# Two of three terms of each gate and up product in one 512-column matmul, with other buffers for the first units

## What is computed

```python
        gu = rmsnorm(h, g_ffn[i]) @ w_gate_up[i]      # (512, 2048) @ (2048, 11264)
        g_, u_ = gu[..., :D_FF], gu[..., D_FF:]
        h = h + (jax.nn.silu(g_) * u_) @ w_down[i]    # (512, 5632) @ (5632, 2048)
```

## Time and profile before

| | us |
|---|---|
| median of three runs (2725.11 to 2725.7) | 2725.15 |
| the profiled execution | 2726.73 |
| its span, first to last instruction | 2724.9 |
| TensorE busy | 2687.5 (99%) |
| VectorE busy | 1818.1 (67%) |
| ScalarE busy | 1187.9 (44%) |
| first to last issue of a gate and up weight load | 1125.3 to 1999.6 |

### The profile page before, as it was taken

The page is one execution under the profiler, slowest core; times in us unless marked ns, Lnnn a source line. Parts: engine busy times, 40 slices in busy tenths (PEclk is TensorE's granted clock), DMA queues, the critical chain, the costliest instruction groups (busy, mean ns, idle before and its releaser), DMA issues.

```text
span 2724.9 us, 42137 instructions
## 1 busy us (share of the span) xinstructions
PE 2687.5 (99%) x17284; PEld 2450.5 (90%) x17284; DVE 1818.1 (67%) x2072; ACT 1187.9 (44%) x1527; POOL 169.7 (6%) x130
## 2 busy tenths in 40 slices
PE   9999999999999999999999999999999999999998
PEld 7888888888888888899999999999998999999887
DVE  6555545455565433587787777777788787788745
ACT  5334434334455233354444444444454353444543
POOL 0000000010000111100000000000000000000052
PEclk9999999999999999999999999999999999999999
DMA  6333333323333554454555555555567564553333
GB/s 219 93 93 108 100 100 108 101 85 113 100 97 101 193 200 121 129 161 148 168 155 155 163 148 155 163 162 148 155 216 252 146 208 124 182 153 112 88 98 100
DMA packets 130454, 382.95 MB, mean 141 GB/s; under 512 B 11120, under 2 KB 37872, under 8 KB 127728
## 3 DMA queue, kind: packets, MB, share of 16 engines
q1 hardware_dynamic: 113824, 333.35, 37.3%
q0 software_dynamic: 9792, 34.61, 6.9%
q10 hardware_dynamic: 6672, 12.63, 1.2%
HBM read 301.90 MB, written 44.04 MB: 127 GB/s over the span
## 4 chain that ended last, share of the span: by engine, by line
PE 92%; DVE 4%; DMA 1%; ACT 1%; issue 1%; POOL 0%; ACTq 0%; DVEq 0%; SPq 0%; POOLq 0%
PE ps L574 30%; PE ps L576 30%; PE ps L575 30%; PE ps L648 1%; DVE arena L1948 1%; ACT w_hi L986 0%; DMA arena<-hid 0%; PE ps L637 0%; DVE w_lo L1941 0%; DVE w_lo L1566 0%; DMA raw<-raw 0%; DVE lo L1941 0%; DVE emb L2277 0%; DVE res L2093 0%; PE ps L615 0%
## 5 line engine op out<-in xcount | busy, mean ns | idle before, releaser
L574 PE MATMUL ps<-arena,w_hi 128*128 128x256 f32 (+1 forms) x4164 | 1365.2, 328 | 11.2 <-DVE w_lo L1941 7.5
L576 PE MATMUL ps<-arena,w_lo 128*128 128x256 f32 (+1 forms) x4164 | 1360.0, 327 | 0.0
L575 PE MATMUL ps<-arena,w_hi 128*128 128x256 f32 (+1 forms) x4164 | 1359.7, 327 | 0.0
L986 ACT ACTIVATE w_hi<-raw 128x1024 fp32r<-128x1024 f32 (+1 forms) x536 | 559.9, 1045 | 933.5 <-PE ps L576 914.1
L574 PEld LDWEIGHTS ps<-arena,w_hi 128*128 128x128 f32 x4164 | 793.7, 191 | 83.9 <-issue 12.1
L576 PEld LDWEIGHTS ps<-arena,w_lo 128*128 128x128 f32 x4164 | 793.4, 191 | 66.8
L575 PEld LDWEIGHTS ps<-arena,w_hi 128*128 128x128 f32 x4164 | 793.7, 191 | 65.1 <-issue 0.2
L1566 DVE TENSOR_TENSOR w_lo<-raw,w_hi 128x1024 fp32r<-128x1024 f32 x212 | 268.4, 1266 | 434.1 <-ACT w_hi L986 433.7
L1941 DVE TENSOR_TENSOR w_lo<-raw,w_hi 128x1024 fp32r<-128x1024 f32 (+1 forms) x318 | 379.0, 1192 | 147.1 <-ACT w_hi L986 145.6
L574 PE MATMUL ps<-arena,hi 128*128 128x256 f32 (+1 forms) x1244 | 355.3, 286 | 11.5 <-DVE lo L1941 10.8
L575 PE MATMUL ps<-arena,hi 128*128 128x256 f32 (+1 forms) x1244 | 354.8, 285 | 0.0
(11 more groups left out here) (174 smaller groups left out, 1821.1 us busy)
## 6 DMA issues: line engine op xcount, KB each, us to landing
raw<-w_gu SPq DMA_DIRECT2D x176, 512.0 KB, 4.1
raw<-w_in SPq DMA_DIRECT2D x108, 512.0 KB, 3.5
raw<-w_dn SPq DMA_DIRECT2D x64, 512.0 KB, 4.4
raw<-raw POOLq DMA_DIRECT2D x60, 512.0 KB, 4.7
hid<-res SPq DMA_DIRECT2D x22, 1024.0 KB, 5.2
raw<-w_o SPq DMA_DIRECT2D x32, 512.0 KB, 3.8
raw<-w_pg SPq DMA_DIRECT2D x32, 512.0 KB, 3.7
arena<-hid SPq DMA_DIRECT2D x14, 1024.0 KB, 8.2
```

Of the source, the lines that this page charges most:

```text
L574: mm(out, hi, x[:, 0, :], start=start, stop=False, skip_group_check=more)
L575: mm(out, hi, x[:, 1, :], start=False, stop=False, skip_group_check=more)
L576: return mm(out, lo, x[:, 0, :], start=False, stop=stop, skip_group_check=more)
L986: return nc.scalar.activation(out, in_, ACT.Copy, scale=scale)
```

## The change

For units below 44 a term k is two matmuls instead of three. The high part of the weights is multiplied by both parts of the moving operand at once: 512 columns, which are two runs of 256 columns in the operand's slot (its high and low part lie 8 KB apart), written to a whole PSUM bank. Its left half then holds high x high, its right half high x low. The low part of the weights times the high part of the operand (256 columns) is added to the right half. So the result is the sum of the two halves of a bank. The snapshots and the two sums take whole banks (1024 elements instead of 512), and VectorE adds right to left in two new steps, `gate_fold` and `up_fold` (512 elements each); scale, Silu and product work on the left halves. The rows that a tile needs in `res` are now all its own until `hidden_tile`, so snapshots of unit u wait for the hidden tile of unit u - 2.

Beside it: slots 0, 7, 5, 1 for even and 2, 3, 4, 6 for odd units, with the loads of unit 0 in the order A21, A22, A11, A12; `gate_scale` moves behind `up_sum`, `up_scale` behind `sum_3`, `recip` behind low part 2 of unit 1, Silu behind high part 3; ScalarE scales its half of x_last ahead of the store of h; at the change to down residual tiles 1 and 2 change places; two of four w_pp loads wait for the last unit's block sum 3. The down units keep `product`.

```diff
-    return (0, 1, 2, 3)[i] if v % 2 == 0 else (5, 7, 4, 6)[i]
+    return (0, 7, 5, 1)[i] if v % 2 == 0 else (2, 3, 4, 6)[i]
...
             def block_load(v, i):
+                if v < 2 and raw_slot(v, i) < RAW:
+                    sp.wait_ge(w_lo_done, N_WO + 29 + raw_slot(v, i))
                 if v == 0:
-                    sp.wait_ge(w_lo_done, N_WO + 29 + i)
+                    if i == A21:
+                        sp.wait_ge(mrg_hi, 8)
                 elif v == 1:
                     if i == A22:
                         sp.wait_ge(acc_done, SQUARES[3])
-                    if i == A21:
-                        sp.wait_ge(mrg_hi, 8)
                     if i == A12:
                         sp.wait_ge(tot_done, 4)
...
                 if v == 0:
-                    for i in (A21, A22, A12):
+                    for i in (A21, A22, A11, A12):
                         block_load(0, i)
-                    for i in (A21, A11, A22, A12):
+                    for i in (A11, A21, A22, A12):
                         block_load(1, i)
...
                 if v == FF + 2:
                     sp.wait_ge(hidden, FF)
-                    residual_again(2)
+                    residual_again(1)
                 if v == FF + 1:
                     sp.wait_ge(hidden, FF - 1)
-                    residual_again(1)
+                    residual_again(2)
...
+            def product_by_parts(out, hi, lo, x, start, stop, more):
+
+                mm(out, hi, x, start=start, stop=False, skip_group_check=more)
+                return mm(out[:, 1], lo, x[:, 0], start=False, stop=stop, skip_group_check=more)
...
-                    i = product(out, hi[:, c], lo[:, c], x[:, :, k], j < 4 and k == 0, k == pairs(v) - 1, j >= 4)
+                    if v < FF:
+                        i = product_by_parts(parts, hi[:, c], lo[:, c], x[:, :, k], j < 4 and k == 0,
+                                             k == pairs(v) - 1, j >= 4)
+                    else:
+                        i = product(out, hi[:, c], lo[:, c], x[:, :, k], j < 4 and k == 0, k == pairs(v) - 1, j >= 4)
...
             def snap_row(u):
                 act.wait_ge(s_used, 7 * u + 3)
+                if u == 1:
+                    act.wait_ge(xs_lo, 22)
                 if u >= 2:
-                    act.wait_ge(ff_sum, 2 * (u - 2) + 2)
+                    act.wait_ge(hidden, u - 1)
                 b = bank0(u)
-                copy(halves(ff_row(u, US)), ps[:, b + DELTA:b + GAMMA + 1, LEFT]).then_inc(snap, 1)
+                copy(up_rows(u), ps[:, b + DELTA:b + GAMMA + 1]).then_inc(snap, 1)
...
-                b = bank0(u)
-                tt(halves(ff_row(u, GG)), halves(ff_row(u, GS)), ps[:, b + BETA:b + GAMMA + 1:2, LEFT],
-                   ALU.add).then_inc(ff_sum, 1)
+                b, g = bank0(u), gate_rows(u)
+                tt(g, g, ps[:, b + BETA:b + GAMMA + 1:2], ALU.add).then_inc(ff_sum, 1)
+
+            def gate_fold(u):
+                dve.wait_ge(ff_sum, 2 * u + 1)
+                g = gate_rows(u)
+                tt(g[:, :, LEFT], g[:, :, LEFT], g[:, :, RIGHT], ALU.add).then_inc(g_folded, 1)
```

More of the change, by code:

```diff
@@ L301, in hid_rows, with gate_rows, up_rows @@
             return res[:, 0:4, :] if u // 2 % 2 == 0 else res[:, 12:16, :]
-        def ff_row(u, i):
-            return res[:, 4 + 4 * (u % 2) + i, :]
-        GS, US, GG, UU = range(4)
+        def gate_rows(u):
+            return res[:, 8 - 4 * (u % 2):10 - 4 * (u % 2), :]
+        def up_rows(u):
+            return res[:, 10 - 4 * (u % 2):12 - 4 * (u % 2), :]
         def halves(row):
@@ L523, in _ @@
                     continue
+                block_load(v, A11)
+                if last_before:
+                    fill(last_before, 2)
                 block_load(v, A12)
@@ L863, in _ @@
             i.then_inc(piece_used, 1)
-            def n_group(g, n, pair):
-                free(g, 4)
-                for j in range(4):
-                    piece(n + j, j, 2 * pair, [n_tile(4 * j + k) for k in range(4)], j == 0, j == 3)
-            def down(g, n, pair0, need):
-                pe.wait_ge(ff_lo, need)
-                for d in range(8):
-                    free(g + d, 4)
-                    piece(n + d, d, 2 * ((pair0 + d) % 4), [r1[:, k] for k in range(4)], True, True)
             def strassen(v, j):
@@ L898, in strassen @@
                 pe.wait_ge(s_lo, n + 1)
-                x, out = x_slot(g, j), ps[:, bank0(v) + BANK_OF[j], X_HALF[0]]
+                x, bank = x_slot(g, j), ps[:, bank0(v) + BANK_OF[j]]
+                out, parts = bank[:, X_HALF[0]], bank.rearrange("p (t c) -> p t c", t=2)
                 hi, lo = S_HI[ring(n)], S_LO[ring(n)]
@@ L1398, in _ @@
                     x_split(T3_, SIX, res[:, 0:6, RIGHT], 0, N_WO + 31)
+                if g == 7:
+                    act.wait_ge(emptied, G_E)
+                    copy(x_last[:, 1, :], res[:, 15, :], gn[:, G_FFN + 15:G_FFN + 16]).then_inc(x_made, 1)
                 h_store(g)
                 if g == 7:
-                    copy(x_last[:, 1, :], res[:, 15, :], gn[:, G_FFN + 15:G_FFN + 16]).then_inc(x_made, 1)
                     hi(0, 2)
@@ L1426, in _ @@
                         nc.scalar.preload_act_table(ACT.Silu)
-                    if j == 2 and v <= FF:
+                    if j == 3 and v <= FF:
                         gate_act(v - 1)
@@ L2055, in up_sum, with up_fold @@
                 dve.wait_ge(s_used, 7 * u + 7)
-                b = bank0(u)
-                tt(halves(ff_row(u, UU)), halves(ff_row(u, US)),
-                   ps[:, b:b + 1, LEFT].broadcast_to([P, 2, 256]), ALU.add).then_inc(ff_sum, 1)
+                b, r = bank0(u), up_rows(u)
+                tt(r, r, ps[:, b:b + 1].broadcast_to([P, 2, SEQ]), ALU.add).then_inc(ff_sum, 1)
+            def up_fold(u):
+                dve.wait_ge(ff_sum, 2 * u + 2)
+                r = up_rows(u)
+                tt(r[:, :, LEFT], r[:, :, LEFT], r[:, :, RIGHT], ALU.add).then_inc(u_folded, 1)
             def up_scale(u):
-                dve.wait_ge(ff_sum, 2 * u + 2)
-                tt(ff_row(u, UU), ff_row(u, UU), rstd[:, 0, :], ALU.mult).then_inc(u_scaled, 1)
+                dve.wait_ge(u_folded, u + 1)
+                r = up_rows(u)[:, :, LEFT]
+                tt(r, r, by_token(0), ALU.mult).then_inc(u_scaled, 1)
             def hidden_tile(u):
@@ L2071, in hidden_tile @@
                     dve.wait_ge(h_out, 16 * 8)
-                tt(hid_row(u, u % 2), ff_row(u, GG), ff_row(u, UU), ALU.mult).then_inc(hidden, 1)
+                tt(halves(hid_row(u, u % 2)), gate_rows(u)[:, :, LEFT], up_rows(u)[:, :, LEFT],
+                   ALU.mult).then_inc(hidden, 1)
             def t_1_3(u):
@@ L2141, in _ @@
                 lo(v, 2)
+                if v == 1:
+                    recip(3, 3, 1, 0, D)
                 if v <= FF:
                     up_sum(v - 1)
+                    gate_scale(v - 1)
                 if v >= FF:
```

35 lines of the change are left out of this document (18 added, 17 removed).

## The result

The changed kernel takes 2697.07 us, the median of seven runs, against 2725.11 for the kernel before beside it: a ratio of 0.9916, 95% interval 0.9902 to 0.993. The forecast was 2693 us, the range 2687 to 2706. But the seven runs are no cloud around one value. Four lie between 2694.91 and 2697.07 us, three between 2711.43 and 2712.08, and none in between. The kernel before has nothing like it (2723.91 to 2726.59). Most of what follows is about these 16 us.

The account below looks back on a forecast made before the run. The prediction took TensorE, busy 99% of 2724.9 us, to bound the kernel. From 2725.15 us, -32.8 (joint matmul) - 1.5 (first units) + 2 (last gate and first down unit) = -32.3 gave 2693 us, range 2687 to 2706.

Parts of the forecast that it names:

- TensorE bounds the stretch, and only its own instructions can shorten it: Gate and up stretch, 1200 to 1980 us: TensorE always busy at full clock, nothing waits on its path.
- Joint matmul, -32.8 us: Units below 44: each of 2464 terms falls from 360.0 to 346.7 ns, one matmul's fixed cost; 32.8 us less.
- rival 1: Joint matmul pays inside where its second operand run begins: 2726 us (3%), or 2720 us with 2.5 ns gained a term (3%).
- starts 0.24 us after a joint matmul: Gate stretch, sign of a wrong forecast: this spacing would point to rival 1; 0.23 would show the forecast right.
- VectorE's new work, 0: Gate and up units: longer sums and two folds stay hidden behind TensorE, VectorE 91 to 93% busy; cost 0.
- Rival 2: VectorE's folds and sums run at full lengths without overlap: 4 to 22 us back, 2697 to 2715 us; 10%.
- Rival 3: VectorE becomes the bound, its two-bank reads and folds at nearly twice the time: 21.5 us a unit, 2784 us; 4%.
- First units, -1.5 us: Units 0 and 1: new slots shorten product (0,2)'s wait, later products wait more; -5.0 + 3.5, bounds -5 and +2.
- the clock probably stays: Unit 0, product (0,2): with its wait cut to 2.1 us the clock no longer falls to half, -2.3 us.
- ScalarE's larger snapshots, 0: Gate and up units: about 1 us more per unit on ScalarE, which has room; cost 0.
- Last gate and first down unit, +2 us: Change to down: VectorE's longer work delays low parts 3 to 6 by 1.1 to 1.7 us; bounds 0 and +5.

Follow-up runs that it names:

- the repeat: The changed kernel timed again with no edit: 2696.39 us, ratio 0.991 to the kernel before.
- pair order: Changed kernel with two 512-column, then two 256-column matmuls by turns inside a product of units 1 to 43: 2701.07 us, ratio 0.9909.
- the buffer kernel: Kernel before with only the change's slots, load order and load waits, earlier x_last copy and later w_pp loads: 2723.21 us, ratio 0.9991.
- eight-and-eight order: Changed kernel with eight 512-column matmuls, then eight of 256 columns, in each product of units 1 to 43: 2703.44 us, ratio 0.9922.

## Why the prediction held, and where it did not

**TensorE bounds the stretch, and only its own instructions can shorten it: right.** With three matmuls and all of the change's other work the term stays at 359.9 ns; with the joint matmul it becomes 346.5 or 353.2.

**Joint matmul, -32.8 us: right in the lower group, twice too much in the upper.** 360.0 - 346.5 = 13.5 ns a term is 33.3 us; 360.0 - 353.2 = 6.8 ns is 16.8. The step that failed is "The cost goes with the instruction itself, not with what follows it, so a mixed row of them can be priced from these". The three starts at the norm's total cross the border of the sizes once each way; they show nothing of a row in which every neighbour differs. Such a row has two paces, and the evidence held only the better. The forecast of 2693 is 2 to 4 us below the lower group and the range holds it, but the upper group, 3 of 7 runs here and 2 of 6 in the repeat, lies 5 to 8 us above the range. That the median came out inside is luck: four of seven runs were of the lower group, and with one more of them in the upper it would have been 2711. The thirteen runs of the changed kernel have a mean of 2702.1.
On the fixed cost of a matmul, the runs give 13.5 ns for one merged pair in the faster pace. The 2.5 ns of the Trainium skill's page "TensorE: Matmul & The Clock Gate" ("Wait — 56ns, not 53.3ns?") would have made the gain 6 us, an estimate from that page, and no run here agrees with that: even the slower pace gives 6.8 ns a term.

**The 2720 and 2726 of the first rival: not seen.** Its mechanism, a price for the second run of the operand, is refuted by the kernel that reads one run and has the same two groups. The loss that did come, half of the gain in some executions, lies between forecast and rival, and no rival described it. The sign that was to point at rival 1, starts 0.24 us after a joint matmul, did show in the upper group, so it did not single that rival out.

**VectorE's new work, 0: right.** The share is 90% in the upper group's profile (695.52 / 760 = 91.5% in the lower), forecast 91 to 93; no product of units 2 to 42 waits in the rows (the 0.1 us at (42,6) is the only delay there). Rival 2, no overlap, is refuted by its timeline in the changed kernel:

```profile
1412.01 1.22 DVE L2056 TENSOR_TENSOR res<-res,ps 128x1024 f32<-128x1024 f32 x1 [0.52 <-PE ps L586]
1413.15 0.42 DVE L2103 TENSOR_TENSOR res<-res 128x256 f32<-128x256 f32 x1
1413.48 1.22 DVE L1950 TENSOR_TENSOR lo<-raw,hi 128x1024 fp32r<-128x1024 f32 x1
```

The gate sum over two whole banks takes 1.22 us and lets the next start after 1.14; the 256-element sum behind it gives 0.33, the value taken. Rival 3 asked for nearly twice that. The upper group could be mistaken for rival 2 by its time alone (2711 lies in its 2697 to 2715); the profile tells them apart, since TensorE never waits in that stretch.

**First units, -1.5 us: sum about right, parts moved.** The chain did what was laid out: ScalarE takes the block sum at 1145.82 (1146.3 forecast) without a wait, the residual tile is at 1151.99, and TensorE starts (0,2) at 1156.77 (1157.6), a wait of 1.2 to 1.6 us where 2.1 stood. (0,5) and (0,6) wait 0.6 us each, where 1.5 was booked for both together and VectorE held to be the cause; the row of (0,6) names ScalarE's snapshot. (The 0.4 us by which product (0,1) was to end sooner was 0.2: two products at 0.1 us less.) (1,3) waits 2.0 to 2.4 (2.5 forecast), but "the clock probably stays" held for unit 0 alone: it falls behind (1,3) instead, which the sum didn't book there. From the start of unit 0 to that of unit 2 it is 49.34 us before (1149.90 to 1199.24), 47.09 in the upper group's profile (1149.81 to 1196.90) and 47.74 in the lower group's (1149.92 to 1197.66). Some 0.8 us of that is the joint matmul's gain in these 112 terms, mostly at the slower pace, so the term is -1.5 and -0.8, inside its bounds of -5 and +2; by the medians the buffers alone gave -2 on the kernel before and 0 beside the joint matmul.

**ScalarE's larger snapshots, 0: right but for the borders.** In the stretch no product waits for one. TensorE's stop ahead of the down units, at (43,6), is one for a snapshot and takes 0.77 us instead of 0.50.

**Last gate and first down unit, +2 us: about +4.** From the start of product (43,1) to that of (46,1) it is 69.85 us before (2028.68 to 2098.53), 73.69 in the upper group's profile (2011.07 to 2084.76) and 73.26 in the lower group's (1996.62 to 2069.88), +3.8 and +3.4, though the 48 joint terms in it save 0.3. TensorE's named stops there add up to 9.0 and 10.4 us, against 6.7 before. The reason that was booked, VectorE's longer work, is there, and one that wasn't. ScalarE's wait for a filled operand is longer now, as its row in the profile of the lower group shows against the earlier trace rows:

```profile
2023.47 1.06 ACT L990 ACTIVATE arena<-arena 128x1024 fp32r<-128x1024 f32 x1 [6.49 <-DMA arena<-hid]
```

```profile
2024.57 1.22 DVE L1957 TENSOR_TENSOR arena<-arena 128x1024 fp32r<-128x1024 f32 x1 [2.29 <-ACT arena L990]
2025.71 1.21 DVE L2072 TENSOR_TENSOR res<-res,ps 128x1024 f32<-128x1024 f32 x1
2026.84 0.68 DVE L2066 TENSOR_TENSOR res<-res,rstd 128x512 f32<-128x512 f32 x1
2027.44 0.42 DVE L2114 TENSOR_TENSOR res<-ps,res 128x256 f32<-128x256 f32 x1
2027.77 1.22 DVE L1950 TENSOR_TENSOR lo<-raw,hi 128x1024 fp32r<-128x1024 f32 x1
```

The operand comes 11.8 us after TensorE's stop ahead of the unit (2011.68), where before it came 10.1 us after it (2053.87 against 2043.74). Its transfers stand in SyncE's queue behind block loads that wait for VectorE, and went out 1.8 us later by the same count (2010.06 against 2040.36). From the operand to the low part's end VectorE then takes 1.14 us more, for the longer up sum and the gate scale. The forecast had let the transfers be "not faster with a faster TensorE" and missed that a fuller VectorE starts them later. The clock falls there too, in the kernel before as in the upper group's profile (0.74 from 2040 to 2060).

**Sum.** By the same fixed starts, lower group: -1.6 for units 0 and 1, -30.5 from (2,0) to (43,1), +3.4 to (46,1) and -1.5 behind it, together -30.2 us between the profiles, 2694.8 against 2724.9. Upper group: -2.3, -15.3, +3.8 and -1.5, together -15.3, 2709.6 against 2724.9. By the medians of the repeat the lower group is 2696.39 - 2726.17 = -29.8. The -1.5 behind (46,1) is not the change's: the same stretch is as long as before in the profile of the kernel with the third term in the left half.

None of the variants beats the changed kernel's lower group. The pair order gives up that group for runs within 4 us of 2701, which is 1 us under the mean of the changed kernel's thirteen runs: no difference that these runs can tell.

## What to carry to other kernels

Where TensorE is the bound and nothing waits, merging two matmuls with the same weights into one of 512 columns saves the fixed cost of one instruction (13.5 ns here, but half of it at the slower pace), and the work that it puts on another engine is free as long as that engine's queue, laid out against TensorE's beats, keeps a margin at every step. Price a new mixture of sizes only from rows of the same mixture, and when runs fall in two groups, compare the counts of matmuls in equal windows: with the clock at 1.00 and no idle time, all that the timeline shows of such a pace is a start 0.01 us later. Changes at the borders of a stage (other buffers, a later sum) mostly moved a wait and the fall of the clock behind it to the next product: count them by the time from one fixed instruction to another, not by the wait that goes.

## What the runs showed of the hardware

- Strictly alternating matmuls of 512 and 256 columns, each with its own weight load, run at 346.5 or at 353.2 ns a pair, at a granted clock of 1.00 in both; the slower is a cycle of three pairs. The pace is kept from one stop of TensorE to the next (800 us in the repeat) and taken up anew at a stop, even at one that costs 0.14 us. With every size in twos or eights, a pair costs 348.2 and 348.9 ns. What picks the pace is open. How often it is the slower one differs from kernel to kernel, 13 of 20 stretches with a stop every second unit, 0 of 11 in the one profile with a stop every fourth.
- A stop for which the row names 0.17 us of idle costs 0.41 us of time.
- A moving operand in two runs 8 KB apart costs a matmul no more than one in one run: both kernels have groups at 2695 and 2712 us and the same 4304 matmuls in the window.
- In the first units the granted clock fell to half behind some waits of about 2 us (2.05 at 1182.52 in the buffer kernel, 1.99 at 1184.00 in the changed one, 2.39 at 1184.91 in its repeat) and not behind those of 1.2 to 1.75 us at the start of unit 0. But the length of the wait doesn't decide it: the clock stayed full behind 2.46 us at 1158.23 in the buffer kernel, 2.35 at 1184.14 in eight-and-eight order, and 2.28 at 1184.76 in the kernel with one run, whose TensorE windows are below. So where the fall comes differs between traces whose waits are nearly alike.

```profile
1180.00:1185.00 5.00, 2.72 (x16) 1.00 0.51 128
1185.00:1190.00 5.00, 5.00 (x29) 1.00 0.18 33
```
